# Four layers of a two-stack transformer: one unrolled instruction flow in place of five blocks with barriers

## What is computed

```python
# first stack, l in 0, 1
hn = rms_norm(h, g_mix[l]);  proj = hn @ w_in[l]          # q, k, v, xr, gr; q and k get a partial rope
o  = rms_norm(diff_attention(q, k, v, lam), g_subln[l]) * (1 - lam_init)
y  = rg_lru(causal_depthwise_conv(xr)) * gelu(gr)
h  = h + concat(o, y) @ w_out[l]
h  = h + square(relu(rms_norm(h, g_mlp[l]) @ w_mlp_in[l])) @ w_mlp_out[l]
h  = h + sigmoid(rms_norm(h, g_ple[l]) @ w_ple_gate[l]) * (p[l] @ w_ple_proj[l])
x  = rms_norm(h, g_final)                                  # the final norm
# second stack, l in 0, 1
proj = rms_norm(x, g_pre_mix[l]) @ w_in[l]                 # u, q, k, v, iq, ik, iw
mix  = concat(pool_mixer(u), dsa_attention(q, k, v, top 128 of 512 by iq, ik, iw)) @ w_out[l]
x    = x + rms_norm(mix, g_post_mix[l])
f    = square(relu(rms_norm(x, g_pre_ffn[l]) @ w_ff1[l])) @ w_ff2[l]
x    = x + rms_norm(f, g_post_ffn[l])
```

## Time and profile before

| | |
|---|---|
| time, median of 3 | 2607.3 us (2605.78 to 2608.44) |
| profiled execution: time / span | 2607.97 / 2606.2 us |
| granted TensorE clock over the span | 0.967 |
| PE busy, weight loads busy | 93%, 75% |
| DVE, ACT, POOL busy | 57%, 32%, 14% |
| DMA | 83 GB/s over the span, queue of loads busy 23.5% of 16 engines |

### The profile page before, as it was taken

The page is one execution under the profiler, slowest core; times in us unless marked ns, Lnnn a source line. Parts: engine busy times, 40 slices in busy tenths (PEclk is TensorE's granted clock), DMA queues, the critical chain, the costliest instruction groups (busy, mean ns, idle before and its releaser), DMA issues. The chain is left out here.

```text
span 2606.2 us, 29311 instructions
## 1 busy us (share of the span) xinstructions
PE 2427.2 (93%) x11390; PEld 1951.3 (75%) x11398; DVE 1483.1 (57%) x2110; ACT 841.4 (32%) x1171; POOL 352.1 (14%) x275
## 2 busy tenths in 40 slices
PE   7999999997998999999798888999969888899996
PEld 5877888886786888888676767888857676788885
DVE  6775454455776644544479747344447975734543
ACT  4554222233445322223332443222223244322221
POOL 1001000010200100001036422000023642200002
PEclk9999999999999999999799999999989999999998
DMA  4211322222121223222121111222221111122222
GB/s 148 103 61 57 113 97 83 96 97 100 61 103 49 83 97 107 96 87 96 52 73 63 65 50 64 97 97 96 97 72 67 65 65 52 62 97 100 96 94 81
DMA packets 33301, 217.75 MB, mean 84 GB/s; under 512 B 4128, under 2 KB 4384, under 8 KB 7840
## 3 DMA queue, kind: packets, MB, share of 16 engines
q1 hardware_dynamic: 33184, 216.18, 23.5%
HBM read 214.07 MB, written 2.10 MB: 83 GB/s over the span
## 5 line engine op out<-in xcount | busy, mean ns | idle before, releaser
L332 PE MATMUL ps<-gh,wh 128*128 128x512 f32 (+1 forms) x1728 | 697.9, 404 | 96.9 <-DVE gl L473 61.6
L332 PE MATMUL ps<-gl,wh 128*128 128x512 f32 (+1 forms) x1728 | 680.3, 394 | 0.0
L332 PE MATMUL ps<-gh,wl 128*128 128x512 f32 (+1 forms) x1728 | 680.1, 394 | 0.0
L307 ACT ACTIVATE wh<-wr 128x2048 fp32r<-128x2048 f32 x196 | 374.1, 1909 | 560.2 <-PE ps L332 560.2
L313 DVE TENSOR_TENSOR wl<-wr,wh 128x2048 fp32r<-128x2048 f32 x176 | 406.1, 2308 | 244.6 <-ACT wh L307 244.6
L332 PE MATMUL ps<-hh,wh 128*128 128x512 f32 x1280 | 504.1, 394 | 2.2 <-ACT arena L704 2.2
L332 PE MATMUL ps<-hh,wl 128*128 128x512 f32 x1280 | 499.3, 390 | 0.0
L332 PE MATMUL ps<-hl,wh 128*128 128x512 f32 x1280 | 499.0, 390 | 0.0
L332 PEld LDWEIGHTS ps<-gh,wh 128*128 128x128 f32 (+1 forms) x1728 | 327.6, 190 | 196.7 <-DVE gl L473 67.4
L332 PEld LDWEIGHTS ps<-gl,wh 128*128 128x128 f32 (+1 forms) x1728 | 328.1, 190 | 72.8 <-issue 5.3
L332 PEld LDWEIGHTS ps<-gh,wl 128*128 128x128 f32 (+1 forms) x1728 | 327.4, 189 | 72.1
(11 more groups left out here) (204 smaller groups left out, 2374.8 us busy)
## 6 DMA issues: line engine op xcount, KB each, us to landing
wr<-in_weights SPq DMA_DIRECT2D x198, 1024.0 KB, 4.7
x<-in_xt SPq DMA_DIRECT2D x1, 2048.0 KB, 12.0
out_yt<-x SPq DMA_DIRECT2D x1, 2048.0 KB, 7.2
tmp<-in_positions SPq DMA_DIRECT2D x4, 256.0 KB, 3.6
arena<-in_gates SPq DMA_DIRECT2D x2, 512.0 KB, 4.9
arena<-in_embed SPq DMA_DIRECT2D x2, 512.0 KB, 5.6
par<-in_params_b SPq DMA_DIRECT2D x2, 274.0 KB, 3.5
par<-in_params_a SPq DMA_DIRECT2D x2, 157.5 KB, 2.7
```

What stands on the lines that cost most here:

```text
L307: act.activation(mem.wh[:, c % 2, :], mem.wr[:, c % 2, :], ACT.Copy).then_inc(sem["high"], 1)
L332: done = pe.matmul(out, stationary, moving, start=(first and n == 0), stop=(last and n == 2), skip_group_check=True)
```

## The change

Both hardware loops over layers, the blocks and all barriers but the one at the end go. The four layers are four `Stage` objects; each engine runs the program of each stage after the other in one block. Two sets of semaphores take turns; POOL clears the set of the stage before in the middle of a stage. The roles of `gh`, `gl` and `hh`, `hl` are swapped from stage to stage, so that the next input can be written while the present one is read. The weight buffers run on over layer borders (`sem.buffer(c)`), and the two chunks of zeros at the end are no longer loaded. Then:

```diff
@@ start, SP of the first stage
+            sp.dma_start(mem.first_gains, gains[0:P, :]).then_inc(shared["gains_loaded"], 16)
+            sp.dma_start(x[:, 0:2, :], slices[:, 0:2, :]).then_inc(shared["x_loaded0"], 16)
+            chunk(0)
+            ... # x[2:4], x[4:6], x[6:8], constants, each its own DMA
+            chunk(1)
@@ start, ACT and DVE of the first stage
+            for k in range(KT):
+                if k % 2 == 0:
+                    act.wait_ge(shared[f"x_loaded{k // 2}"], 16)
+                input_high(act, stage, k)
+                if k == 1:
+                    split_high(act, mem, sem, 0)
+            split_high(act, mem, sem, 1)
...
+            split_low(dve, mem, sem, 0)
             for k in range(KT):
                 gain_low(dve, mem, sem, 0, k, mem.first_gains)
+            ... # idb and trib cast, then
+            split_low(dve, mem, sem, 1)
@@ SP of a later stage
+            chunk(0)
+            chunk(1)
+            chunk(2)
+            stage.after_before(sp)     # x of the stage before is finished
             sp.dma_start(tmp[:, 0, :].bitcast(I32), positions).then_inc(sem["positioned"], 16)
@@ end of a layer of A, ACT (following = the next stage)
+                split_high(act, following.mem, following.sem, 0)      # ahead of the last two tiles
             for t in range(2):
+                n = 2 * (c - A_GATE) + t
                 act.wait_ge(sem["drained"], A_TILE[c] + t + 1)
                 act.activation(tmp[:, 1, :], tmp[:, 0, :], ACT.Sigmoid).then_inc(sem["gate_out"], 1)
+                act.wait_ge(sem["finished"], n + 1)
+                input_high(act, following, n)
+        split_high(act, following.mem, following.sem, 1)
@@ end of a layer of A, DVE
                 drain(tmp[:, 0, :], A_TILE[c] + t)
+                if n:
+                    gain_low(dve, following.mem, following.sem, 0, n - 1, mem.first_gains)
                 dve.wait_ge(sem["gate_out"], n + 1)
                 own.mark(dve.tensor_tensor(tmp[:, 1, :], tmp[:, 1, :], proj[:, n, :], ALU.mult))
                 own.settle()
-                own.mark(dve.tensor_tensor(x[:, n, :], x[:, n, :], tmp[:, 1, :], ALU.add))
+                dve.tensor_tensor(x[:, n, :], x[:, n, :], tmp[:, 1, :], ALU.add).then_inc(sem["finished"], 1)
+        gain_low(dve, following.mem, following.sem, 0, KT - 1, mem.first_gains)
+        split_low(dve, following.mem, following.sem, 1)
@@ end of a layer of B, DVE
             own.mark(scaled_branch(k, BP_FPOST, k % 4))
-            scaled_branch(k + 1, BP_FPOST, k % 4 + 1).then_inc(sem["branch_scaled"], 1)
             own.settle()
-            own.mark(dve.tensor_tensor(x[:, k, :], x[:, k, :], tmp[:, k % 4, :], ALU.add))
+            dve.tensor_tensor(x[:, k, :], x[:, k, :], tmp[:, k % 4, :], ALU.add).then_inc(sem["finished"], 1)
+            scaled_branch(k + 1, BP_FPOST, k % 4 + 1).then_inc(sem["branch_scaled"], 1)
+            if following and k:
+                for i in (k - 2, k - 1):
+                    gain_low(dve, following.mem, following.sem, 0, i, mem.first_gains)
@@ first_two_chunks: paired only within a layer of B, and in its start where the norm is not folded
-    for k in range(KT // 2):
+    for k in range(KT):
         before(k)
         part(k, 0)
+        if paired and k < KT // 2:
             part(k, 1)
-    ...
-    sum_squares(pe, mem, sem, n)
+    sums()
+    for k in range(KT // 2 if paired else 0, KT):
         part(k, 1)
         if k == KT - 3:
-            spread_root(pe, mem, sem, n)
+            spreads()
@@ final norm, folded into the first layer of B (folded = layer == 0)
+            dve.tensor_tensor(mem.first_gains, mem.first_gains, cst[:, C_GFIN:C_GFIN + KT], ALU.mult)
+        act.activation(mem.normed_sq[:, k % 2, :], mem.x[:, k, :], ACT.Square, scale=cst[:, C_GFIN + k:C_GFIN + k + 1])
+        ... # POOL gathers both kinds of squares; PE sums both (32 matmuls of one column)
+            raw = mean of x²; root = raw ^ -0.5                                  # DVE, POOL
+            mean = root² * (sum of (g x)²) / D + EPS; its root; diag of root * second root; spread
+            dve.wait_ge(sem["spread"], 1)
+            diagonals(dve, mem, root).then_inc(sem["raw_diag"], 1)
+                pe.wait_ge(sem["raw_diag"], 1)
+                pe.wait_ge(sem["kept"], 1)
+                pe.matmul(ps[:, 5, :], cst[:, C_ONES:C_ONES + P], tmp[:, 3, :], ...)   # kept by ACT as raw_root
@@ attention steps s of that layer, DVE, ahead of maxima(s + 2)
+            if folded and s < KT:
+                dve.scalar_tensor_tensor(out=x[:, s, :], in0=x[:, s, :], scalar=cst[:, C_GFIN + s:C_GFIN + s + 1],
+                                         in1=raw_root, op0=ALU.mult, op1=ALU.mult)
@@ end of the last layer, SP
+            for k in range(KT):
+                sp.wait_ge(sem[("finished", "added")[k % 2]], k // 2 + 1)
+                sp.dma_start(out.rearrange("(k p) s -> p k s", p=P)[:, k, :], x[:, k, :]).then_inc(shared["stored"], 16)
```

## The result

The changed kernel takes 2561.25 us (median of 4 runs, 2556.86 to 2563.96) where the kernel before takes 2607.35: a ratio of 0.9822, 95% interval 0.9805 to 0.9839. It is 46 us faster. The forecast was 66.2 us and its range ended at 2557, so the time lies 4 us outside it.

A forecast was written before the change was run, and what follows sets the result against it. PE was taken to bound the kernel, leaving 179 us of its idle time; 6.4 + 15.7 + 33.3 − 1.5 + 9.8 + 2.5 = 66.2 us off 2607.3 gave 2541.1 us, 8 times in 10 within 2532 to 2557.

The forecast's parts named there:

- Part 1: Start: PE's first product at about 12.4 in place of 18.77 us, 6.4 us saved, bounds 4.4 to 8.
- Part 2: Border of the A layers: PE goes on without a gap or slow start, 15.7 us saved, bounds 12 to 15.7.
- Part 3: Final norm folded ahead of stack B: 33.3 us saved, bounds 27 to 35; then 1.5 lost rewriting x in attention.
- Part 4: Border of the B layers: first product 11.6 us earlier, less 1.8 for late root and drain, 9.8 saved, bounds 7 to 12.5.
- Part 5: End: seven slices stored while later ones are computed, 2.5 us saved, bounds 0 to 4.5.
- (b): Rival: DVE and POOL hold each other up in the tail ahead of stack B; 2551 to 2557 us, chance 0.15.
- The rewrite of x: B's attention stage: two of eight added DVE operations on the path, 1.5 us lost, bounds 0 and 7.8.
- (a): The forecast itself, 2541 us, between 2532 and 2551 by its own bounds, chance 0.72.
- (d): Rival: a wait kept in order holds the root back at each of three borders, 5 us each; 2556 to 2565, chance 0.06.
- (c): Rival: free rewrite of x and earlier loads at the start save 75 us; 2532 and below, chance 0.05.
- (e): Rival: instructions of the doubled, fresh layer code come too late, so slower; 2678 us at 6 ns each, chance 0.02.
- No idle time over 1 us at the two borders behind A layers: Sign of being right: no such PE idle time there up to the spread, with the clock staying 1.00.

The follow-up runs named there:

- e8: Changed kernel with ACT's weight split ahead of the update wait, a reordered start and a reordered border between the B layers: 2540.31 us, ratio 0.9749.
- e1: Changed kernel with ACT's weight-chunk split in the A tails moved right behind the second sigmoid, ahead of its wait for the update: 2546.43 us, ratio 0.9764.
- e3: Changed kernel without the folded norm's second kind of squares, their adds and sums: 2553.74 us (one run).
- e4: Changed kernel with a tiny ACT copy before the wait for x and DVE's first two low parts ahead of its chunk 0 split: 2558.81 us, ratio 0.9813.
- e2: Changed kernel with POOL's adds of squares in the A tails cut to 8 of 512 columns, order unchanged: 2558.33 us, ratio 0.9815.

## Why the prediction was wrong

**The sum was right for another order.** Forecast by part, against the changed kernel and e8, by the same marks (us saved in the profiled run):

| | forecast | after | e8 |
|---|---|---|---|
| Part 1, start | 6.4 | 3.8 | 6.3 |
| Part 2, A/A (with the rest of A1) | 15.7 | 8.8 | 15.7 |
| Part 3, A/B and attention | 31.8 | 21.7 | 32.7 |
| Part 4, B/B (with the rest of B1) | 9.8 | 5.5 | 7.6 |
| Part 5, end | 2.5 | 4.5 | 4.5 |
| sum | 66.2 | 44.3 | 66.9 |

That e8 meets Part 3 and the sum within 1 us is partly luck. e1 has the same order there and gives 29.1 in Part 3: 1.6 us of the difference are the clock from 1260 to 1273 and 2.0 the clock in attention (231.65 us against e8's 229.67 for the same instructions). Parts 1 and 4 of e8 have orders that the forecast didn't have.

**Parts 2 and 3: the step that failed** is "In those 5.4 us DVE does ... 4.0 us. ACT does ... under 3 us. Both fit". It is a sum of work, and it was nearly right as that: in a turn of two tiles, 12.09 us, DVE was idle for 3.12 + 0.19 + 0.29 us. But the two engines hand on to each other six times a turn through queues kept in order, and I didn't follow the order: drain, sigmoid, product, update, high part, square, the same without the drain for the second tile, split, low part, next drain. Laid end to end that ring is 12.09 us, and 11.37 with every product undisturbed, longer than PE's 10.9. The overlap with PE that Parts 2 and 3 took for granted was not there. The "four tiles of slack" of the banks don't help, since what PE lacks is a weight chunk and not a bank. The trace of before had all the durations; what was missing was to write the two queues side by side. With the split moved (e1) Part 2 is exact. In front of stack B the ring was longer by ACT's second squares (0.71 each) and POOL's adds of them, 13.73 us a turn; without them it is 12.1 and the first gap 2.82 for 4.10 (e3). Part 3's own terms held: PE's wait for the second diagonal was forecast at 0.8 and is 0.78 (1289.28 in the trace after); a term of about 0.3 us was left out, the first drain's wait, 1.09 against 0.81 before.

**The bounds.** "12 to 15.7" for Part 2 was drawn from the root at the border alone; no bound was given for a tail that is slower than PE. Parts 1, 2 and 4 gave less than their lower bounds (3.8, 8.8 and 5.5 for 4.4, 12 and 7). The range 2532 to 2557 had room for rival (b)'s some 10 us in the tails and not for the 15 that the two borders missed.

**The rewrite of x** was put at 1.5 us on the path with bounds 0 and 7.8. It cost nothing that shows: the lead over before was 34.03 us ahead of attention (first product of the third chunk, 1328.27 against 1294.24) and 34.3 behind it, with a clock of 0.95 over this stretch in both profiles.

**Part 1** had the first product at 12.4 and it came at 14.48. The table load of 1.28 us was left out, which the earlier trace rows show at the start of a layer and which stands behind the wait for x here. And the low part of slice 0, in the sum at 0.75, took 1.75 (12.67 to 14.42), since POOL's add ran until 13.88. With both put ahead e4 gets 11.95. Another 0.5 us is lost behind the first product: 23.13 us from there to the first norm's mark, 22.62 before.

**Part 4** was right up to the first product: PE's gap was forecast as about 7 us and is 6.63. The root was to be 1 us late and is 1.68. The drain's wait behind it was to cost "as much once more" and costs 1.9 more than before (2.70 against 0.81). Behind that wait another 1.9 us is lost up to the next norm's mark (231.87 us for 229.94), which is about the clock: 0.87 over the 13 us from 1937 on, where before had 1.00 behind its own wait of 0.81 (1980 to 1993). The other profiles with the two waits show 0.87 or less in the same place, but e4's shows 1.00, and there this stretch takes 228.74 us. So my forecast had a mechanism right and the clock left out.

**Part 5**: the end gave 4.5 for 2.5. The last slice is added until 2558.27 and the span ends at 2561.9, 3.6 us later; I had 3.6 + 0.4 for the store and 1.1 more for the clear. The mis-sized term is the landing: the eight stores of 256 KB took 2.0 us each (median), not the 3.6 of the positions. The bounds from the earlier trace rows (0 to 4.5) just held it, but I took a middle value where each term lay beside another.

**The rivals.** (b) forecast the time, 2551 to 2557, better than (a), but for the wrong place and cause. Its test was mine: low parts over 1.3 us are there, yet e2 shows that POOL's adds are worth 2.9 us at most. (d) is nearest in kind, a wait kept in order, and its range holds the time. I looked for it at the borders, for positions and loads, and not in the tail. (c) and (e) are out. For (e): A1 is where the kernel before runs a loop's second pass and the changed kernel new code. From A1's second mark to its last 350.91 us lie before (881.16 to 1232.07) and 350.90 after (868.57 to 1219.47); from its first to its second 209.27 before and 209.24 to 209.32 in the six profiles without a dip of the clock there. So the new code costs nothing that shows. "No idle time over 1 us at the two borders behind A layers" was the sign that I named, and it is what failed.

**DVE beside POOL.** I read the row of 1.31 us against 0.75 as a lock that is felt "less than half". That was a misreading, since the add in question began ahead of it. In the tails, at the border B/B and at the end, a DVE operation over 512 columns with two operands in SBUF that starts while POOL adds ends 0.55 us behind POOL's end, whatever its own start; from the trace after, the end of the program:

```profile
2548.04 1.70 POOL L1480 TENSOR_TENSOR x<-x,tmp 128x512 f32<-128x512 f32 x1 [5.74 <-DVE tmp L1792]
2548.66 1.63 DVE L1863 TENSOR_TENSOR x<-x,tmp 128x512 f32<-128x512 f32 x1
...
2551.03 1.70 POOL L1480 TENSOR_TENSOR x<-x,tmp 128x512 f32<-128x512 f32 x1 [1.29 <-DVE tmp L1792]
2551.65 1.63 DVE L1863 TENSOR_TENSOR x<-x,tmp 128x512 f32<-128x512 f32 x1
```

POOL ends at 2549.74 and DVE at 2550.29, then 2552.73 and 2553.28. In the turn above DVE's product (616.89, 1.41 us) ends 0.54 behind POOL's add (until 617.76). All 22 such pairs in these places of the trace after keep to it, and the three low parts of weight chunks (2048 columns) that start beside an add in front of stack B end 2.15 us behind it. So does the row that I misread: POOL's add before it ran from 19.66 to 20.98 in the kernel before, and the low part of the earlier trace rows ends at 21.54, 0.56 behind it. The Trainium skill's rule in "SBUF — State Buffer", section "SBUF: two separate sides", that the pair is an exclusive lock which the loser waits for in full, agrees with these rows. That the rival built on it was still wrong has another reason: what the waits for POOL add to a turn is 0.72 us in A0 and 1.12 in A1 (e2), and the ring is longer than PE's turn without them.

## What to carry to other kernels

When work is moved beside other work, don't ask only whether each engine's sum fits: write down the queues in order, follow the hand-overs around until the chain comes back to its start, and compare the length of that ring with the bottleneck's turn. An operation that depends on nothing but a load (a split of weights, a table load) must not stand in a queue behind a wait for something computed. And compare two traces by marks that both have; the loss then shows its stretch at once.

## What the runs showed that I had not expected

The clock falls after short waits, but not each time: to 1.2 GHz for most of 3.7 us behind an idle time of 2.60 us. Behind the waits of 1.68 and 2.70 us at the border B/B (over 13 us that start 4.4 us behind the spread) the mean was 0.87 in the first profile of the changed kernel and 0.74 in the second, 0.87 in four of the other kernels that have these waits, and 1.00 in e4's alone. In A1, from 830 to 868 us, three profiles (the two of the changed kernel and e3's) had 0.96, and the six others had 1.00 over the same instructions. In B0's attention the same instructions took from 227.3 to 231.8 us, at 0.98 to 0.95. A stretch of this kind is worth 1.5 to 4.5 us, and the changed kernel's runs differ by 7 us. A difference of 2 or 3 us between two totals here says little; the marks around the edited place say more. I can't say from these runs what decides it.
